# Where a decoder step splits its attention output, and where the taps of a short convolution stand on the vector engine

## The chip, the cores and the metric

The kernel runs on one core of one Trainium2 chip. The metric is the device time of one execution in microseconds (us), the median of several runs. TensorE does matrix products and transposes, VectorE (DVE) and ScalarE (ACT) do elementwise work, GpSimd (POOL) a little of it, and SyncE (SP) issues nearly all transfers. Each engine takes its instructions strictly in the order in which they are written, and semaphores order one engine against another.

## The reference, cut to what matters

One inference step of a two-layer decoder trunk, for 512 prompt tokens and 8 x 4 sample tokens (544 columns in all), everything in float32. Each layer is a feed-forward half step, a mixer, and a second feed-forward half step:

```
x = LN(alpha*x + 0.5*SwiGLU_1(x))
f_r, f_s, f_g = split(x @ W_in)          # 2696 columns: 22 chunks of 128
x = LN(alpha*x + W_out[concat(RWKV7(f_r), SWA(f_s), GDN(f_g))])
x = LN(alpha*x + 0.5*SwiGLU_2(x))
```

SWA is windowed attention (8 query heads). RWKV7 has 4 heads, taken in two pairs; GDN, a gated delta rule, has 4 heads in two more pairs. GDN's q, k and v go through a causal convolution over four tokens first:

```
conv = full[:, 0:T] * conv_w[0]
for j in range(1, 4): conv = conv + full[:, j:j+T] * conv_w[j]
q, k, v = split(silu(conv))
```

Each pair of heads then builds a 128 x 128 triangular system per token tile, inverts it, and runs a recurrence over the four tiles of 128 tokens.

## The kernel before

Activations lie with features on partitions and the 544 tokens along the free axis. Every float32 product of the large matrices is done as three products of a high and a low part (`xh`, `xl` of the activations, `wh`, `wl` of the weights). ACT makes the high part by a copy, DVE the low part by a subtraction.

The mixer of a layer starts with the projection: 22 chunks, each one weight block (`proj_chunk` on ACT and DVE, `proj_part` on TensorE). The steps of the prompt's attention are spread between the chunks; the last of them, `values(7)`, leaves the attention output `y_attn` complete two chunks before the end. Between the last two chunks ACT does two Tanh on `proj[:, 6]` (`lora_t`), which DVE then turns into the operand `lora` of the first products of RWKV (`zw`, `a_mm`).

After the projection comes `head_pairs`. Four pairs of heads, q = 0 to 3 (0 and 1 are RWKV, 2 and 3 are GDN), go through `prepare(q)` and `finish(q)`. Both are Python generators, one pair per engine, and `alternate` lays the steps of two of them into one program: the samples' attention (`samples_attend`, 7 steps) beside `prepare(0)`, then `prepare(q + 1)` (32 steps for q + 1 = 1, 30 for 2 and 3) beside `finish(q)` (22 steps). What stands in which step therefore decides the order on an engine; nothing is reordered on the chip.

Two places matter here.

1. The split of `y_attn` (128 x 2048). On ACT the copy to `xh` (`attn_h`) stands in the first step of `samples_attend`, on DVE the subtraction into `xl` (`attn_l`) does too. With the interleaving that is after `prepare(0)` has asked for the sum of squares `kk_sum`: on ACT behind the Ln and Exp of `rsqrt`, on DVE ahead of `newton`, whose first instruction (it ticks `kk_read`) lets TensorE go on with the third of the four `cum` products (L940). `y_attn` lies in the space that `prepare(0)` later uses for its tiles R_ to KT_; so only the exponentials of `cum` wait for `attn_l`.

2. The four taps of GDN's convolution (`tap(0)` to `tap(3)` in `prepare_gdn` on DVE; each is three instructions on about 512 columns and three on 32). Taps 0 to 2 stand in the first step of `prepare_gdn`, tap 3 at the head of the second. Also in the first step TensorE does the 4 `cum` and 16 `dif` products of the pair; behind them, in its own first step of `finish`, stand the first products of the recurrence (for q = 1), for whose result DVE's copy `cx` (L2328) waits. For q = 2 that copy is L2322 and waits for nothing that TensorE does here. ACT's Tanh (`conv_t`) wait for the whole convolution, and what follows from it (`conv_s`, the squares, `qk_sum`, `rsqrt`, `newton`, the grams, the inverse) is a chain through all three engines.

Of the kernel before, what the change touches and what calls it, by code (L numbers as in the profile page):

```python
# [17 lines left out]
F32 = mybir.dt.float32  # L18
# [242 lines left out]
def trunk(nc, A, O, layers=DEPTH):  # L261

    with ExitStack() as ctx:
# [106 lines left out]
        def region(o, w):  # L370
            return ar[:, o:o + w], o + w

        M_NORM = M_WORK + 6 * NT
        ck, _ = region(M_TMP, DEC_BATCH * P)
        y_attn, _o = region(M_TMP, 4 * NT)
        kd, _o = region(_o, 2 * NT)
        vt, _o = region(_o, TILES * P)
        ko, _o = region(_o, P)
        stat, _o = region(_o, 40)
        assert _o <= M_NORM  # L380
        vn, _o = region(M_NORM, DEC_BATCH * P)
# [935 lines left out]
        def _(act):  # L1317
# [91 lines left out]
            def one_layer(lay):  # L1409
# [61 lines left out]
                for g in range(PC):  # L1471
                    proj_chunk(g)
                    if g == FIRST_SHIFTED - 1:
                        double_keys()
                    if g == FIRST_ACTION - 2:
                        caches()
                    for action, s in actions_of(g + 1):
                        take(action, s)
                    if g == PC - 2:
                        act.wait_ge(sem("shifted"), at(lay, "shifted", 7))  # L1480
                        go(proj[0:32, 6, :], proj[0:32, 6, :], ACT.Tanh).then_inc(*tick("lora_t"))
                        go(proj[64:128, 6, :], proj[64:128, 6, :], ACT.Tanh, scale=0.5).then_inc(*tick("lora_t"))

                def samples_attend():

                    act.wait_ge(sem("proj_d"), at(lay, "proj_d", PC))
                    go(xe[:, :, :, 3:7], proj[:, GCH:GCH + 6, SEQ:NT].rearrange("p c (b t) -> p c b t", b=DEC_BATCH)).then_inc(*tick("xe"))
                    act.wait_ge(sem("y_copied"), at(lay, "y_copied", HALVES))
                    go(xh[:, 2:6, 0:SEQ], y_attn[:, :, 0:SEQ]).then_inc(*tick("attn_h"))
                    act.wait_ge(sem("tail_t"), at(lay, "tail_t", 3))  # L1490
# [45 lines left out]
                def prepare_rwkv(p):  # L1536
                    q, c, U, lwt = p.q, p.c, p.U, p.lwt
                    act.wait_ge(sem("attn_out"), at(lay, "attn_out", 32))
                    act.wait_ge(sem("ys"), at(lay, "ys", 1))
                    if q:  # L1540
                        act.wait_ge(sem("attn_l"), at(lay, "attn_l", 2))
                    if q == 1:
# [12 lines left out]
                    act.wait_ge(sem("cum"), at(lay, "cum", q + 1))  # L1555
                    act.wait_ge(sem("attn_l"), at(lay, "attn_l", 1))
                    go(U[:, 0:3, 0:SEQ].rearrange("p k (i n) -> p k i n", i=TILES),
# [216 lines left out]
        def _(dve):  # L1774
# [133 lines left out]
            def one_layer(lay):  # L1908
# [118 lines left out]
                for g in range(PC):  # L2027
# [6 lines left out]
                    for action, s in actions_of(g + 1):  # L2034
                        take(action, s)

                ts(par("a0h"), par("a0"), 0.5, None, ALU.mult, None).then_inc(*tick("ys"))
                ts(par("kah"), par("k_a"), 0.5, None, ALU.mult, None).then_inc(*tick("d_seq"))
# [4 lines left out]
                def samples_attend():  # L2043

                    dve.wait_ge(sem("qm_zero"), at(lay, "qm_zero", 1))
                    for h in range(8):
                        dve.tensor_copy(qm_d[64 * (h // 4):64 * (h // 4) + 64, :, h % 4 * 4:h % 4 * 4 + 4],
                                        proj[64 * (h % 2):64 * (h % 2) + 64, SCH + h // 2, SEQ:NT].rearrange("p (b t) -> p b t", b=DEC_BATCH)).then_inc(*tick("qm"))
                    dve.wait_ge(sem("attn_h"), at(lay, "attn_h", 1))
                    tt(xl[:, 2:6, 0:SEQ], y_attn[:, :, 0:SEQ], xh[:, 2:6, 0:SEQ].bitcast(F32), ALU.subtract).then_inc(*tick("attn_l"))  # L2050
                    yield
# [71 lines left out]
                def prepare_rwkv(p):  # L2123
# [3 lines left out]
                    dve.wait_ge(sem("attn_out"), at(lay, "attn_out", 32))  # L2127
                    if q:
                        dve.wait_ge(sem("attn_l"), at(lay, "attn_l", 2))
                    if q == 1:  # L2130
# [44 lines left out]
                def prepare_gdn(p):  # L2175
# [25 lines left out]
                    dve.wait_ge(sem("xe"), at(lay, "xe", 1))  # L2201
                    for k in range(3):
                        tap(k)
                        dve.wait_ge(sem("d_seq"), last(lay, "d_seq"))
                    yield
                    tap(3)
                    dve.wait_ge(sem("dif"), at(lay, "dif", 2 * c + 1))
                    for n in range(2):
                        ts(gram[:, 4 * n:4 * n + 4, 2 * P:3 * P], ps[:, 2 + n, :].rearrange("p (m n) -> p m n", m=4), 0.0, None, ALU.min, None).then_inc(*tick("dif_min"))
                    yield  # L2210
                    dve.wait_ge(sem("dif"), at(lay, "dif", 2 * c + 2))
                    ts(gram_s[:, :, 2 * NSAMP:3 * NSAMP], ps[0:NSAMP, 1, 0:2 * NSAMP].rearrange("p (m n) -> p m n", m=2), 0.0, None, ALU.min, None).then_inc(*tick("dif_min"))
                    yield
                    for n in range(3):
                        dve.wait_ge(sem("dif_e"), at(lay, "dif_e", 3 * c + n + 1))
                        gr, wd, mask = (gram[:, 4 * n:4 * n + 4], P, cst("gmask")) if n < 2 else (gram_s, NSAMP, cst("gmask_s", NSAMP))
                        for k in (1, 0):
                            tt(gr[:, :, (2 + k) * wd:(3 + k) * wd], gr[:, :, 2 * wd:3 * wd],
                               bc(mask[:, k * wd:(k + 1) * wd].rearrange("p (o n) -> p o n", o=1), [wd, gr.shape[1], wd]), ALU.mult).then_inc(*tick("d_seq"))
# [351 lines left out]
```

## Time and profile before

| | us |
|---|---|
| median of 3 runs | 2966.72 |
| lowest and highest of them | 2965.29, 2972.21 |
| the profiled execution | 2972.21 |
| its span in the trace | 2970.4 |
| mean granted clock of TensorE | 0.912 |

The profiled execution took 1.8 us more than its span and is the slowest of the three runs, 5.5 us over the median. The granted clock is given as a part of full speed: 1.0 is 2.4 GHz and 0.5 is 1.2 GHz, and a value between is a stretch with both. In the trace the mixer of the first layer runs from 606 to 1073 us and that of the second from 2070 to 2534 us; layer 1 is the second one in what follows, layer 0 the first.

### The profile page before, as it was taken

How to read it: one execution, taken by the hardware profiler on the slowest of the kernel's cores; microseconds unless marked ns; L12 is line 12 of the kernel's file. 1: busy time of each engine (PE TensorE's matmuls, PEld its weight loads, DVE VectorE, ACT ScalarE, POOL GpSimd, SP SyncE). 2: the span in 40 equal slices, each digit the busy share in tenths (PEclk: the TensorE clock that was granted, in tenths of full speed). 3: DMA queues.
4: the chain of work that ended last, by engine and by line, in shares of the span. 5: the costliest groups of instructions: out<-in, count | busy, mean ns of one | idle time of the engine just before them, and what ended most of it. 6: DMA issues, size and time to landing. Idle time of an engine off the chain costs nothing.

```text
span 2970.4 us, 59212 instructions
## 1 busy us (share of the span) xinstructions
PE 2726.1 (92%) x23222; PEld 2548.2 (86%) x23222; DVE 1668.4 (56%) x2503; ACT 947.0 (32%) x1694; POOL 161.1 (5%) x168
## 2 busy tenths in 40 slices
PE   8999999879796989999999999998887778999997
PEld 8999998866665889999999999987666667999996
DVE  5666347744646466663366653566445654666534
ACT  4333233422212243332233332343122222433323
POOL 1030110000000010001100001100000000100011
PEclk9999999976767999999999999999767779999998
DMA  4842334100000322232232222431000012223221
GB/s 113 101 91 87 89 103 128 44 27 1 9 9 1 95 68 86 85 90 86 76 88 87 85 86 87 119 101 51 7 1 9 9 42 73 79 86 90 82 87 60
DMA packets 380501, 201.67 MB, mean 68 GB/s; under 512 B 41461, under 2 KB 376821, under 8 KB 379528
## 3 DMA queue, kind: packets, MB, share of 16 engines
q1 hardware_dynamic: 377928, 197.46, 23.1%
q0 software_dynamic: 2400, 1.82, 1.9%
q8 instruction: 118, 1.93, 0.3%
q14 instruction: 55, 0.45, 0.0%
HBM read 188.07 MB, written 13.34 MB: 68 GB/s over the span
## 4 chain that ended last, share of the span: by engine, by line
PE 78%; DVE 10%; issue 5%; ACT 4%; DMA 1%; SPq 1%; DVEq 0%; POOLq 0%; ACTq 0%; POOL 0%
PE ps L682 52%; PE ps L737 25%; DVE ar L1920 3%; ACT ar L1415 2%; DVE ar L1914 2%; DVE wl L1798 1%; ACT wh L1346 1%; SPq L529 1%; PE ps L1011 1%; DVE x L1914 1%; DMA raws<-in_ffn_w_in 0%; DVE xl L1905 0%; DVE ar L1950 0%; DVE ar L1917 0%; DMA raws<-in_w_in 0%
## 5 line engine op out<-in xcount | busy, mean ns | idle before, releaser
L1798 DVE TENSOR_TENSOR wl<-raws,wh 128x1024 fp32r<-128x1024 f32 x336 | 411.2, 1225 | 671.1 <-ACT wh L1346 666.8
L737 PE MATMUL ps<-ar 64*64 64x64 f32 (+13 forms) x5408 | 508.7, 287 | 127.3 <-ACT ar L1415 39.0
L682 PE MATMUL ps<-xh,wh 128*128 128x272 f32 x2880 | 604.5, 291 | 19.9 <-DVE wl L1798 17.4
L682 PE MATMUL ps<-xh,wl 128*128 128x272 f32 x2880 | 599.5, 290 | 0.0
L682 PE MATMUL ps<-xl,wh 128*128 128x272 f32 x2880 | 598.0, 289 | 0.0
L737 PEld LDWEIGHTS ps<-ar 64*64 64x64 f32 (+6 forms) x5408 | 380.8, 172 | 231.1 <-issue 71.3
L1346 ACT ACTIVATE wh<-raws 128x1024 fp32r<-128x1024 f32 x336 | 354.8, 1057 | 416.3 <-PE ps L682 375.4
L682 PEld LDWEIGHTS ps<-xh,wh 128*128 128x128 f32 x2880 | 457.0, 190 | 23.0 <-DVE wl L1798 19.4
L682 PEld LDWEIGHTS ps<-xl,wh 128*128 128x128 f32 x2880 | 457.3, 190 | 0.0
L682 PEld LDWEIGHTS ps<-xh,wl 128*128 128x128 f32 x2880 | 456.8, 190 | 0.0
L682 PE MATMUL ps<-hh,wh 128*128 128x272 f32 x1408 | 292.2, 289 | 0.0
L682 PE MATMUL ps<-hl,wh 128*128 128x272 f32 x1408 | 290.4, 287 | 0.0
L682 PE MATMUL ps<-hh,wl 128*128 128x272 f32 x1408 | 290.1, 287 | 0.0
L1415 ACT ACTIVATE ar<-ps 64x256 f32<-64x256 f32 (+19 forms) x250 | 91.2, 392 | 481.5 <-PE ps L737 379.4
L682 PEld LDWEIGHTS ps<-hl,wh 128*128 128x128 f32 x1408 | 222.1, 188 | 0.0
L737 PE MATMUL ps<-xh,wh 128*128 128x272 f32 (+1 forms) x896 | 204.3, 310 | 18.4 <-DVE xl L1914 13.3
L682 PEld LDWEIGHTS ps<-hh,wl 128*128 128x128 f32 x1408 | 219.8, 188 | 0.0
L682 PEld LDWEIGHTS ps<-hh,wh 128*128 128x128 f32 x1408 | 219.7, 188 | 0.0
L737 PE MATMUL ps<-xl,wh 128*128 128x272 f32 (+1 forms) x896 | 190.6, 295 | 0.0
L737 PE MATMUL ps<-xh,wl 128*128 128x272 f32 (+1 forms) x896 | 190.3, 294 | 0.0
L737 PEld LDWEIGHTS ps<-xh,wh 128*128 128x128 f32 x896 | 146.5, 196 | 37.0 <-issue 28.4
L1375 ACT ACTIVATE hh<-work 128x544 f32 (+1 forms) x88 | 58.0, 660 | 370.4 <-DVE work L1862 370.4
(188 smaller groups left out, 2735.5 us busy)
## 6 DMA issues: line engine op xcount, KB each, us to landing
raws<-in_ffn_w_in SPq DMA_DIRECT2D x176, 512.0 KB, 3.7
raws<-in_ffn_w_out SPq DMA_DIRECT2D x64, 512.0 KB, 4.0
raws<-in_w_in SPq DMA_DIRECT2D x42, 512.0 KB, 3.7
raws<-in_ffn_w_out SPq DMA_DIRECT2D x32, 384.0 KB, 3.4
raws<-in_w_out SPq DMA_DIRECT2D x16, 448.0 KB, 4.0
x_kept<-x SPq DMA_DIRECT2D x2, 2176.0 KB, 10.1
x<-x_kept SPq DMA_DIRECT2D x2, 2176.0 KB, 8.0
ar<-in_consts SPq DMA_DIRECT2D x2, 1337.5 KB, 6.7
```

The costliest lines, as they stand in the source:

```text
L529: sp.dma_start(dst, src, allow_slow_non_contiguous=slow).then_inc(*tick(name, 16))
L682: ins = pe.matmul(ps[:, bank + h, 0:n1 - h * NH], w[u % 2][:, k, :], a[:, k0 + k, h * NH:n1], start=(first and k == 0 and n == 0), stop=(l ...
L737: return pe.matmul(dst, lhsT, rhs, start=start, stop=stop, **kw)
L1011: ins = pe.transpose(ps[0:w, i % 4, s * P:(s + 1) * P], src[:, o:o + w], ident)
L1346: act.activation(wh[u % 2][:, :, :], raw[u % 2][:, :, :], ACT.Copy).then_inc(sem("wh_done"), 1)
L1375: act.activation(chunk(hh, i * 2 + u), work[:, 2 + u, :], ACT.Copy).then_inc(sem("hh_done"), 1)
L1415: return act.activation(dst, src, fn, **kw)
L1798: dve.tensor_tensor(wl[u % 2][:, :, :], raw[u % 2][:, :, :], wh[u % 2][:, :, :].bitcast(F32), ALU.subtract).then_inc(sem("wl_done"), 1)
L1914: return dve.tensor_tensor(out, a, b, op)
L1920: return dve.scalar_tensor_tensor(out=out, in0=a, scalar=x, in1=b, op0=o1, op1=o2)
```

## The change

The change has three parts. `y_attn` gets a place of its own further up in memory (what is saved is that it no longer shares space with the cached keys `ck`; it now overlaps the tiles BT to GATE of `prepare(0)`, and the first step of `prepare(0)` waits for `attn_l` on both engines). The split of `y_attn` moves from `samples_attend` to directly behind the projection, on ACT ahead of the two Tanh of `lora_t`, which move there as well, and on DVE ahead of the three small scalings and of `lora`. And the taps of GDN's convolution are spread over four steps.

```diff
@@ regions @@
-        ck, _ = region(M_TMP, DEC_BATCH * P)
-        y_attn, _o = region(M_TMP, 4 * NT)
+        ck, _o = region(M_TMP, DEC_BATCH * P)
         kd, _o = region(_o, 2 * NT)
...
         stat, _o = region(_o, 40)
+        y_attn, _o = region(_o, 4 * NT)
@@ ACT, projection @@
                     for action, s in actions_of(g + 1):
                         take(action, s)
-                    if g == PC - 2:
-                        act.wait_ge(sem("shifted"), at(lay, "shifted", 7))
-                        go(proj[0:32, 6, :], proj[0:32, 6, :], ACT.Tanh).then_inc(*tick("lora_t"))
-                        go(proj[64:128, 6, :], proj[64:128, 6, :], ACT.Tanh, scale=0.5).then_inc(*tick("lora_t"))
+
+                act.wait_ge(sem("y_copied"), at(lay, "y_copied", HALVES))
+                go(xh[:, 2:6, 0:SEQ], y_attn[:, :, 0:SEQ]).then_inc(*tick("attn_h"))
+                act.wait_ge(sem("shifted"), at(lay, "shifted", 7))
+                go(proj[0:32, 6, :], proj[0:32, 6, :], ACT.Tanh).then_inc(*tick("lora_t"))
+                go(proj[64:128, 6, :], proj[64:128, 6, :], ACT.Tanh, scale=0.5).then_inc(*tick("lora_t"))
@@ ACT, samples_attend @@
-                    act.wait_ge(sem("y_copied"), at(lay, "y_copied", HALVES))
-                    go(xh[:, 2:6, 0:SEQ], y_attn[:, :, 0:SEQ]).then_inc(*tick("attn_h"))
@@ ACT and DVE, prepare_rwkv @@
-                    if q:
-                        act.wait_ge(sem("attn_l"), at(lay, "attn_l", 2))
+                    act.wait_ge(sem("attn_l"), at(lay, "attn_l", 1 if q == 0 else 2))
...
-                    act.wait_ge(sem("attn_l"), at(lay, "attn_l", 1))
@@ DVE, projection and samples_attend @@
+                dve.wait_ge(sem("attn_h"), at(lay, "attn_h", 1))
+                tt(xl[:, 2:6, 0:SEQ], y_attn[:, :, 0:SEQ], xh[:, 2:6, 0:SEQ].bitcast(F32), ALU.subtract).then_inc(*tick("attn_l"))
                 ts(par("a0h"), par("a0"), 0.5, None, ALU.mult, None).then_inc(*tick("ys"))
...
-                    dve.wait_ge(sem("attn_h"), at(lay, "attn_h", 1))
-                    tt(xl[:, 2:6, 0:SEQ], y_attn[:, :, 0:SEQ], xh[:, 2:6, 0:SEQ].bitcast(F32), ALU.subtract).then_inc(*tick("attn_l"))
@@ DVE, prepare_gdn @@
-                    for k in range(3):
-                        tap(k)
-                        dve.wait_ge(sem("d_seq"), last(lay, "d_seq"))
-                    yield
-                    tap(3)
+                    tap(0)
+                    yield
+                    dve.wait_ge(sem("d_seq"), last(lay, "d_seq"))
+                    tap(1)
                     dve.wait_ge(sem("dif"), at(lay, "dif", 2 * c + 1))
...
                     yield
+                    dve.wait_ge(sem("d_seq"), last(lay, "d_seq"))
+                    tap(2)
                     dve.wait_ge(sem("dif"), at(lay, "dif", 2 * c + 2))
...
                     yield
+                    dve.wait_ge(sem("d_seq"), last(lay, "d_seq"))
+                    tap(3)
                     for n in range(3):
                         dve.wait_ge(sem("dif_e"), at(lay, "dif_e", 3 * c + n + 1))
```

The rows that follow are the instructions of an engine in program order, with the semaphore that one waits for behind it.

The first place is VectorE where the projection ends and `prepare(0)` begins, before the change. The 64x544 row is `lora`, the one behind it the first product of `prepare(0)`; TensorE waits for `lora`.

```order
L1914 TENSOR_TENSOR ar<-ar,work 128x544 [waits proj_e]
L1917 TENSOR_SCALAR ar<-ar 128x2 x3
L1917 TENSOR_SCALAR ar<-ar 64x544 [waits lora_t]
L2127 ISA
L1917 TENSOR_SCALAR ar<-ar 128x544 [waits attn_out]
```

And with the change:

```order
L1912 TENSOR_TENSOR ar<-ar,work 128x544 [waits proj_e]
L2035 REGISTER_ALU
L1912 TENSOR_TENSOR xl<-ar,xh 128x4x512 [waits attn_h]
L1915 TENSOR_SCALAR ar<-ar 128x2 x3
L1915 TENSOR_SCALAR ar<-ar 64x544 [waits lora_t]
L2125 ISA
L1915 TENSOR_SCALAR ar<-ar 128x544 [waits attn_l,attn_out]
```

The low half of the attention output, `xl`, now stands ahead of `lora`. Before, it stood ahead of the instruction that ticks `kk_read`, the one that waits for `rs_exp`:

```order
L2047 COPY ar<-ar 64x8x4 x7
L1914 TENSOR_TENSOR xl<-ar,xh 128x4x512 [waits attn_h]
L2075 REGISTER_ALU
L1920 SCALAR_TENSOR_TENSOR ar<-ps,ar 128x544 [waits rs_exp]
L1920 SCALAR_TENSOR_TENSOR ar<-ar 128x544 [waits kk_read]
```

The second place is ScalarE at the same point, with the change. The xh row is the copy of the attention output, the two behind it are the Tanh of `lora_t`, which stood one projection chunk earlier before.

```order
L1425 REGISTER_ALU
L1415 ACTIVATE ar<-ar,cols 128x544 [waits proj_n]
L1480 ISA
L1415 ACTIVATE xh<-ar 128x4x512 [waits y_copied]
L1482 ISA
L1415 ACTIVATE ar<-ar 32x544 [waits shifted]
L1415 ACTIVATE ar<-ar 64x544
L1538 ISA
L1539 ISA [waits attn_out]
L1415 ACTIVATE ar<-ar 128x544 [waits attn_l,ys]
```

What moved is again the 128x4x512 operation, to ahead of everything that `prepare(0)` asks for.

The third place is VectorE in `prepare(2)` beside `finish(1)`, with the change. The COPY from ps is the recurrence's `cx`, the row above it the last of tap 0; before, the fifteen rows of taps 1 and 2 and their waits stood between these two.

```order
L1915 TENSOR_SCALAR ar<-ar 128x512
L1915 TENSOR_SCALAR ar<-ar 128x32
L2324 REGISTER_ALU [waits state_out]
L2328 COPY ar<-ps 128x128 [waits cx]
L2201 REGISTER_ALU
L1918 SCALAR_TENSOR_TENSOR ar<-ar 128x511 [waits d_seq]
L1918 SCALAR_TENSOR_TENSOR ar<-ar 128x32
```

All of taps 1, 2 and 3 now stands behind the copy; of the old order only tap 3 did.

## Rows read from the trace of the kernel before

**Rows 1.** The page's first part: busy time of each engine, share of the span.
```profile
PE 2726.1 (92%) x23222; PEld 2548.2 (86%) x23222; DVE 1668.4 (56%) x2503; ACT 947.0 (32%) x1694; POOL 161.1 (5%) x168
```

**Rows 2.** Stretches: mixer of layer 0; prepare(2) of either layer. Length, busy times, clock.
```profile
core 0: us, PE busy (x) PEld busy (x) DVE busy (x) ACT busy (x) POOL busy (x), PEclk, DMA share, GB/s
606.00:1073.60 467.60, 383.02 (x3947) 309.22 (x3948) 245.94 (x512) 120.62 (x220) 12.23 (x9) 0.74 0.09 24
794.60:899.20 104.60, 86.18 (x905) 66.56 (x905) 57.08 (x125) 23.83 (x46) 0.00 (x0) 0.66 0.03 7
2258.80:2356.80 98.00, 78.62 (x905) 60.95 (x905) 56.40 (x125) 23.83 (x46) 0.00 (x0) 0.74 0.03 7
```

**Rows 3.** Chain of waits behind layer 1's projection: start us, length us, what.
```profile
2072.41 3.83 PE ps L737 x14
...
2082.22 1.79 ACT xh L1415
...
2086.24 0.72 DVE ar L1920
2087.01 3.57 PE ps L737 x6
```

**Rows 4.** Timeline of VectorE there: start us, us, line, operation, idle before.
```profile
2071.59 1.30 DVE L1917 TENSOR_SCALAR ar<-ar 128x2 f32<-128x2 f32 x5
...
2084.03 2.29 DVE L1914 TENSOR_TENSOR xl<-ar,xh 128x2048 fp32r<-128x2048 f32 x1 [2.37 <-ACT xh L1415]
```

**Rows 5.** Timeline of ScalarE there.
```profile
2066.36 1.32 ACT L1415 ACTIVATE ar<-ar 32x544 f32<-32x544 f32 x2
...
2072.36 0.73 ACT L1415 ACTIVATE ar<-ar 128x544 f32<-128x544 f32 x1
...
2082.11 1.89 ACT L1415 ACTIVATE xh<-ar 128x2048 fp32r<-128x2048 f32 x1
```

**Rows 6.** TensorE's cum products: layer 0 (the first two rows), then layer 1.
```profile
618.82 1.75 PE L737 MATMUL ps<-ar 128*128 128x386 f32 x4
623.40 1.01 PE L737 MATMUL ps<-ar 128*128 128x386 f32 x1 [2.84 <-DVE ar L1920]
...
2081.38 1.46 PE L737 MATMUL ps<-ar 128*128 128x386 f32 x4
```

**Rows 7.** One stretch there, same columns as in Rows 2.
```profile
2080.00:2084.00 4.00, 2.85 (x17) 1.64 (x15) 1.44 (x9) 3.99 (x5) 0.00 (x0) 0.96 0.00 0
```

**Rows 8.** Timeline of VectorE in prepare(2) of layer 0.
```profile
797.05 5.16 DVE L1920 SCALAR_TENSOR_TENSOR ar<-ar 128x511 f32<-128x511 f32 x12
803.70 0.29 DVE L2328 COPY ar<-ps 128x128 f32<-128x128 f32 x1 [1.48 <-PE ps L737]
803.90 2.55 DVE L1920 SCALAR_TENSOR_TENSOR ar<-ar 128x509 f32<-128x509 f32 x6
...
810.98 2.63 DVE L1920 SCALAR_TENSOR_TENSOR ar<-ar 128x544 f32<-128x544 f32 x4
```

**Rows 9.** Timeline of TensorE there.
```profile
795.25 8.01 PE L737 MATMUL ps<-ar 128*128 128x256 f32 x40 [5.84 <-DVEq L2200]
803.10 0.56 PE L737 MATMUL ps<-raws,gram_odd 128*128 128x64 f32 x4
```

**Rows 10.** Chain of waits behind it: start us, length us, what.
```profile
811.74 1.30 ACT ar L1415 x2
813.04 0.14 issue
813.18 3.98 PE ps L737 x8
...
820.80 1.30 DVE ar L1920
```

**Rows 11.** Timeline of TensorE in prepare(3) of layer 0.
```profile
899.92 9.71 PE L737 MATMUL ps<-ar 128*128 128x256 f32 x54 [5.84 <-DVEq L2200]
```

**Rows 12.** VectorE there.
```profile
907.00 0.23 DVE L2322 COPY ar<-ar 128x128 f32<-128x128 f32 x1
...
909.61 1.28 DVE L1917 TENSOR_SCALAR ar<-ps 128x512 f32<-128x512 f32 x2
```

**Rows 13.** TensorE from 908.4 us on, by form: count, busy us, mean ns.
```profile
L737 PE MATMUL ps<-ar 128*128 128x128 f32 x1 | 0.3, 275 | 0.0
```

More of the change, by code:

```diff
@@ L2127, in prepare_rwkv @@
                     dve.wait_ge(sem("attn_out"), at(lay, "attn_out", 32))
-                    if q:
-                        dve.wait_ge(sem("attn_l"), at(lay, "attn_l", 2))
+                    dve.wait_ge(sem("attn_l"), at(lay, "attn_l", 1 if q == 0 else 2))
                     if q == 1:
```

## The prediction

> **What bounds the kernel now.** I read the busy times first, then the chain of waits, then the timelines of the three engines where the change puts its hand, and the granted clock by stretches last. TensorE is busy for 92% of the span [rows 1], so over the whole run it is the bound. But the change touches only the mixers, and there the picture is another: the mixer of layer 0 takes 467.6 us at a mean granted clock of 0.74, with TensorE busy 383 of them and VectorE 246 [rows 2]. No engine is full; what sets the time is one chain through TensorE, ACT and DVE. The reader should see in [rows 3] and [rows 10] that pieces of all three engines follow each other without a hole, so that whatever is put ahead of one of them on its own engine is paid in full, and what is put beside them is free.
>
> **Part one: the split of the attention output.** Before, the chain behind layer 1's projection goes: DVE makes `lora`, TensorE starts `zw` at 2072.41, and later ACT's copy `attn_h` (1.79 us), DVE's `attn_l` behind it, DVE's 0.72 us that tick `kk_read`, and TensorE's third `cum` product at 2087.01 [rows 3]. Both large operations are on the path there. After, they are on the path earlier. ACT is free for `attn_h` at 2072.36, where it now starts its next operation [rows 5]. `attn_l` starts 1.92 us after `attn_h` (2084.03 - 2082.11) [rows 4, 5] and holds DVE for 2.21 us, until the next start at 2086.24 [rows 3, 4]. From the first of the small scalings to the start of `zw` it is 0.82 us (2072.41 - 2071.59) [rows 3, 4]. The two Tanh, 1.32 us together [rows 5], now come behind `attn_h` and end near 2075.5, hidden by `attn_l`, which ends near 2076.5. So `zw` starts at 2072.36 + 1.92 + 2.21 + 0.82 = 2077.3, which is 4.9 us late. Nothing else for TensorE stands ahead of `zw` in its queue, so it idles.
>
> Against that the later delay goes. In layer 1 TensorE had done the first two `cum` products at 2081.38 + 1.46 = 2082.84 and waited to 2087.01 [rows 3, 6]. Without the split `kk_read` follows the Exp, which ended before `attn_h` began at 2082.11 [rows 5], so 0.72 us later TensorE is no longer kept waiting: it goes on at 2082.84 + 4.9 = 2087.7, a net loss of 0.7 us. In layer 0 the first two end at 618.82 + 1.75 = 620.57 and the third starts at 623.40 [rows 6]; it will start at 625.5, a net loss of 2.1. Together +2.8 us. The ACT wait on `attn_l` that now stands at the head of `prepare(0)` holds up a Square of 0.73 us [rows 5], which ends at 2077.2 and is wanted only after `zw` and `a_mm` (3.83 us [rows 3]): hidden. The copies of the samples' last rows come later in absolute time, but so does all that wants them.
>
> The price has two ends. If the wait for `kk_read` were replaced by another of the same length, the 4.9 us of both layers stay: +9.8. If the products behind it run faster, it is less. The first two products (772 columns) took 1.46 us, the rest with 876 columns 3.57 [rows 3, 6]: the second group ran at the lower level (1.2 GHz), the first at the upper (0.96 granted in that stretch [rows 7]). TensorE stood still between them. Without that pause the rest may keep the upper level and take 1.8 less in each layer: +2.8 - 3.6 = -0.8, and somewhat more if the next products keep it too, so -4 at the low end. I take +2.8, the rows as they stand.
>
> The Trainium skill (TensorE: Matmul & The Clock Gate, Part 4: PE-mode transpose) says that transposes do not count as work that lifts TensorE's clock. Ahead of these `cum` products stand sixteen transposes, so by that rule they would run low after the change, and +2.8 holds. The row of the stretch with transposes and `cum`, 0.96 granted, does not bear the rule out here; without it the sum would lean to -0.8.
>
> **Part two: the taps.** For q = 2, layer 0: TensorE starts `cum` and `dif` at 795.25 and ends them at about 803.1, where the first product of the recurrence follows [rows 9]. DVE meanwhile did tap 0 (until 797.05) and taps 1 and 2 (5.16 us, until 802.2), idled 1.48 us, copied `cx` at 803.70 and went on with tap 3 at 803.90 [rows 8]. Three taps were hidden by TensorE. After, the copy stands behind tap 0, and it can't come earlier than 803.70, since TensorE's order is the same and so are its operands. DVE idles from 797.05 to 803.70, and taps 1 and 2 are done behind it. From 803.90 to 810.98, when `conv_s` begins, DVE has no idle time at all: [rows 8] give the first and the last operation of that stretch, and each of those between begins where the one before it ends. So `conv_s` begins 5.16 us late. It is on the chain: ACT's squares follow at 811.74, TensorE's sums at 813.18, ACT's `rsqrt`, DVE's `newton` at 820.80 [rows 10]. The recurrence does not gain from it, since its copies and its state update on DVE stand at the same steps as before and behind more work. +5.16 us.
>
> For q = 3 the copy `cx` waits for nothing of TensorE's in this stretch; before, it stood at 907.00 behind the taps [rows 12], after 5.16 us earlier. But its reader on TensorE stands behind the same `cum` and `dif`, started at 899.92 [rows 11]: at 908.4 the last `dif` product of 0.275 us is still running [rows 13], so `dif` is ready at about 908.55. Before, DVE took it up at 909.61, behind tap 3 [rows 12]; after, it takes it up at 908.6, 1.0 us earlier, having done only taps 0 and 1 and idled some 4 us. Taps 2 and 3 (2.58 and 2.55 [rows 8]) then come behind. Net +5.1 - 1.0 = +4.1 us. By the bounds of the moment at which `dif` is ready (908.2 to no gain at all) 3.7 to 5.1.
>
> Nothing covers these: ACT's Tanh wait for the whole convolution, and DVE does the masks meanwhile as before. Both layers: 2 x (5.16 + 4.1) = +18.5 us, bounds 17.8 and 20.6.
>
> **The sum.** +18.5 + 2.8 = +21.3 us. The profiled execution took 2972.2, so it would take 2993.5. It lies 5.5 over the median of the runs; on the median, 2966.7 + 21.3 = 2988.0 us, slower by 0.7%.
>
> **What the clock may add.** The same `prepare(2)` with `finish(1)`, the same 905 products, took 104.6 us at a granted clock of 0.66 in layer 0 and 98.0 at 0.74 in layer 1 [rows 2]. So the phase in which TensorE's activity meets the clock is worth 6.6 us in one layer's stretch, and any shift throws that die anew. I count 6.6 us either way as the noise of one such stretch.
>
> **The rivals.**
> A: the clock falls further. TensorE now waits 5 us longer at six places (before `zw`, and before the sums of q = 2 and 3, in two layers). For it: after such waits these rows show low stretches (0.66 and 0.74 over `prepare(2)`). Against it: TensorE was at the lower level behind these waits already. If all stretches of `prepare(2)` lose another 0.08 in both layers, that is 2 x 6.6 on top: 3001 us. The Trainium skill (TensorE: Matmul & The Clock Gate, Why this matters for your kernels) states that rule, that gaps between matmul bursts take TensorE back to the lower clock; it speaks against this change, and the trace agrees in kind.
> B: the taps cost nothing on balance. The state copy of q = 3 comes 5.1 us earlier; if the recurrence rather than the convolution set the time of that stretch, q = 3 would win what q = 2 loses: 2966.7 + 2.8 = 2969.5, no measurable change. For it: DVE's copies of the recurrence do lie on the chain elsewhere. Against it: TensorE is in `dif` until 908.5 whatever DVE does, and the chain runs through the squares and sums [rows 10]. A part of the same case is that the change does not do what it says: that DVE is not reordered on the chip as written; the order of the program leaves no room for it.
> C: faster. The one mechanism is the clock: 0.08 more of it gave 6.6 us. To go under 2957.8, 30 us must come back, 15 in a layer, that is a granted clock up by 0.18 in `prepare(2)` of both (0.84 and 0.92), or the like spread over `prepare(3)`. At 0.90 in both stretches it would be 20 + 13 us back: 2955. It decides only from a clock of some 0.88 on, and with longer pauses nothing points there.
>
> **How the numbers follow.** The forecast, 2988, gets 0.72, with a range of its own from 2974 (18.5 - 4 - 7 above the median) to 2996; A 0.16; B 0.08; C 0.04. The range that should hold 8 in 10 reaches from 2973 to 3003, leaving out B, C and the tail of A. 0.3% of the time, 8.9 us, is about what a measurement of this kernel can tell from no change: faster 0.04 (C), within it 0.09 (B and the lowest part of the forecast), slower 0.87.
>
> **What would show it.** Right: `zw` starts 7.3 us instead of 2.5 behind the last projection product; TensorE's wait inside `cum` is gone; DVE idles about 6.6 us ahead of the copy at L2328 in `prepare(2)` and about 4 us ahead of the two minima in `prepare(3)`, where it idled 1.5 and 0; `conv_s` of q = 2 begins 19.1 us behind the end of tap 0, where it was 13.9 (797.05 to 810.98). Wrong: if the idle time before `cx` is short, TensorE was not the releaser; if all that is there and the time is still below 2975, the clock rose, and the stretches' granted clock must say so; if the total is over 3003, look for stretches below 0.66.

## The result and the profile after

The changed kernel takes 3005.4 us (median of 4 runs, 2995.5 to 3008.2), the kernel before 2966.0 in the same comparison (4 runs, 2962.7 to 2972.2): +39 us, ratio 1.0125, 95% interval 1.0096 to 1.0153, so slower by some 1.3%. The forecast was +21 us. The profiled execution took 3005.6 us, its span is 3003.8, 33.4 us more than the span of the profiled execution before.

Busy times, which answer to [rows 1]:

```profile
PE 2742.8 (91%) x23222; PEld 2561.6 (85%) x23222; DVE 1669.7 (56%) x2503; ACT 949.2 (32%) x1694; POOL 161.5 (5%) x168
```

TensorE does the same 23222 products and is busy 16.7 us longer with them. DVE and ACT gain 1 and 2 us. So about half of the 33.4 us between the two profiled executions is not waiting but slower products.

The stretches answering to [rows 2] (columns as there), mixer of layer 0 and prepare(2) of either layer:

```profile
606.00:1087.00 481.00, 386.59 (x3946) 312.40 (x3946) 245.93 (x512) 122.34 (x221) 11.93 (x9) 0.72 0.08 23
794.60:906.00 111.40, 88.11 (x905) 68.28 (x905) 56.90 (x125) 24.32 (x46) 0.00 (x0) 0.64 0.03 6
2272.90:2384.00 111.10, 88.11 (x905) 68.32 (x905) 56.57 (x125) 24.32 (x46) 0.00 (x0) 0.64 0.03 6
```

Both layers now take 111 us at 0.64, where before one took 104.6 at 0.66 and the other 98.0 at 0.74. They have become equal: the slow one, plus the 5.0 us of later work shown below, plus another 1.5 to 1.8.

TensorE behind layer 0's projection and then layer 1's, answering to [rows 3, 6] (start, length, what, idle before):

```profile
613.21 4.74 PE L737 MATMUL ps<-ar 32*128 32x128 f32 x14 [7.44 <-DVE ar L1915]
...
623.53 3.15 PE L737 MATMUL ps<-ar 128*128 128x386 f32 x10
```

```profile
2091.17 4.74 PE L737 MATMUL ps<-ar 32*128 32x128 f32 x14 [7.44 <-DVE ar L1915]
...
2101.50 3.15 PE L737 MATMUL ps<-ar 128*128 128x386 f32 x10
```

`zw` starts behind a wait of 7.44 us. The ten `cum` records (of which the prediction's first two products are four) run through in 3.15 us, with no wait inside.

VectorE in prepare(2), answering to [rows 8]:

```profile
803.73 0.29 DVE L2328 COPY ar<-ps 128x128 f32<-128x128 f32 x1 [6.73 <-PE ps L737]
803.94 2.56 DVE L1918 SCALAR_TENSOR_TENSOR ar<-ar 128x511 f32<-128x511 f32 x6
...
810.40 2.54 DVE L1918 SCALAR_TENSOR_TENSOR ar<-ar 128x509 f32<-128x509 f32 x6
...
815.96 2.63 DVE L1918 SCALAR_TENSOR_TENSOR ar<-ar 128x544 f32<-128x544 f32 x4
```

The idle time ahead of the copy is 6.73 us (1.48 before). The last row is `conv_s`: 815.96, before 810.98, at equal start of the stretch.

VectorE and TensorE in prepare(3), answering to [rows 11, 12]:

```profile
906.71 8.12 PE L737 MATMUL ps<-ar 128*128 128x256 f32 x54 [5.84 <-DVEq L2197]
...
913.72 1.29 DVE L1915 TENSOR_SCALAR ar<-ps 128x512 f32<-128x512 f32 x2 [2.64 <-PE ps L737]
```

The minima come 7.0 us behind TensorE's start (9.7 before) and `cum` and `dif` take 8.12 us instead of 9.71.

**A ledger by product.** Both traces hold the same 23222 products in the same order, so the starts of each one can be subtracted. The lag of the changed kernel, counted from the first product of each trace, is 0.9 us in layer 0's projection, -0.4 at the head of prepare(2) (TensorE's wait ahead of `cum` and `dif`), 4.6 at the sums of q = 2, 6.4 at the head of prepare(3), 8.7 at the recurrence's product behind the third tap there, and 13.3 at the mixer's end; the FFN adds 0.1. In layer 1 the same six places read 13.4, 13.4, 18.3, 26.8, 29.0 and 32.2. The steps of 5.0 and 2.3 us are later work on VectorE. The rest of the loss stands in two stretches. The first goes from the first sum of q = 2 to the last product ahead of prepare(3)'s wait, 823 records; the second from that recurrence's product of q = 3 to the first one behind the mixer. Here they are for the kernel before, layer 0 and 1, first stretch and then second, and under it the same four of the changed kernel:

```profile
813.20:893.90 80.70, 72.82 (x823) 55.15 (x823) 35.86 (x78) 16.37 (x31) 0.00 (x0) 0.66 0.04 9
2277.40:2351.50 74.10, 65.21 (x823) 49.50 (x823) 35.24 (x78) 16.41 (x31) 0.00 (x0) 0.76 0.04 9
914.10:1121.70 207.60, 177.69 (x1672) 158.69 (x1673) 112.09 (x175) 64.71 (x104) 13.38 (x9) 0.88 0.21 62
2371.70:2580.80 209.10, 179.58 (x1672) 159.34 (x1673) 112.08 (x175) 64.70 (x104) 13.21 (x9) 0.86 0.21 61
```

```profile
818.10:900.60 82.50, 74.63 (x822) 56.78 (x823) 35.86 (x78) 16.37 (x31) 0.00 (x0) 0.63 0.04 8
2296.10:2378.60 82.50, 74.66 (x822) 56.83 (x823) 35.87 (x78) 16.37 (x31) 0.00 (x0) 0.63 0.04 8
923.10:1135.40 212.30, 182.92 (x1672) 161.88 (x1673) 112.48 (x175) 64.60 (x103) 13.40 (x9) 0.85 0.21 60
2401.10:2613.40 212.30, 182.84 (x1672) 161.81 (x1673) 112.40 (x175) 64.61 (x103) 13.39 (x9) 0.85 0.21 60
```

The reader should see that length and granted clock go together (74.1 at 0.76, 80.7 at 0.66, 82.5 at 0.63), while DVE and ACT are busy as long as ever. This is where the surplus over the forecast is. The experiments ask why. Each length is that of one profiled execution.

### The profile page after: what moved, and what is told of

The parts are those of the page before. It is cut to its first block, busy times and chain, and to the rows that moved or that the text cites. A ratio compares the mean times of both kernels' runs of the same rounds, so it can differ in the third digit from the quotient of the medians.

```text
span 3003.8 us, 59208 instructions
## 1 busy us (share of the span) xinstructions
PE 2742.8 (91%) x23222; PEld 2561.6 (85%) x23222; DVE 1669.7 (56%) x2503; ACT 949.2 (32%) x1694; POOL 161.5 (5%) x168
## 4 chain that ended last, share of the span: by engine, by line
PE 78%; DVE 10%; issue 5%; ACT 4%; DMA 1%; SPq 1%; DVEq 0%; POOLq 0%; ACTq 0%; POOL 0%
PE ps L682 51%; PE ps L737 25%; DVE ar L1918 3%; DVE ar L1912 2%; ACT ar L1415 2%; DVE wl L1796 1%; ACT wh L1346 1%; SPq L529 1%; PE ps L1011 1%; DVE x L1912 1%; DMA raws<-in_ffn_w_in 0%; DVE xl L1903 0%; DVE ar L1948 0%; ACT xh L1415 0%; DMA raws<-in_w_in 0%
## 5 line engine op out<-in xcount | busy, mean ns | idle before, releaser
L737 PE MATMUL ps<-ar 64*64 64x64 f32 (+13 forms) x5408 | 517.6, 292 | 146.3 <-ACT ar L1415 39.0
L737 PEld LDWEIGHTS ps<-ar 64*64 64x64 f32 (+6 forms) x5408 | 388.7, 177 | 250.2 <-issue 71.8
L737 PE MATMUL ps<-xh,wh 128*128 128x272 f32 (+1 forms) x896 | 204.1, 310 | 18.4 <-DVE xl L1912 13.3
```

The costliest lines, as they stand in the source:

```text
L737: return pe.matmul(dst, lhsT, rhs, start=start, stop=stop, **kw)
```

## The experiments

All ratios are to the kernel before, run beside them; a ratio of 1.001 is 3.0 us. "First stretch" and "second stretch" are those above, layer 0 / layer 1 of the profiled run.

**The change taken apart.** e1 is the change without the spread taps (that is, `y_attn` in its own place and the early split), e2 the spread taps alone; e3 and e4 spread the taps in one head pair (code shortened):

```
+ late = c == 0        # e3; e4: c == 1
  tap(0)
+ if not late: tap(1), tap(2) here, tap(3) behind the yield, as before
+ else: tap(1), tap(2), tap(3) one behind each of the next yields, as changed
```

e1: 

> The kernel before with the early split of the attention output alone (part one), the taps where they were. Theory T (the loss is all in the taps; the split is free): 2966 +- 4 us, with zw about 4.9 us later and the wait for kk_read gone, net -1.3 to 0 us in each layer as in the profile of the changed kernel. The prediction's own term: +2.8 us, 2969. Rival S (the longer wait ahead of zw also costs granted clock): +8 us or more, 2974 and up, with more time at the lower level behind zw.


Measured 1.0010 [0.9999, 1.0021]; first stretch 74.1 / 74.0. The split is nearly free, +3 us with an interval from 0 to 6. S, which wanted 8 or more, falls.

e2: 

> The kernel before with the spread taps alone (part two). Theory T: as slow as the changed kernel, 3000 to 3008 us, the clock lower as there (0.901 against 0.912). Rival S (part of the clock's loss hangs on the split's wait ahead of zw): 2985 to 2995. The prediction's own term, path alone: 2966 + 18.5 = 2984.5.


Measured 1.0127 [1.0109, 1.0145]; 82.5 / 82.5, second stretch 212.3 / 212.4. The whole loss is in the taps. S falls again.

e3: 

> The taps spread in prepare(2) alone. Path alone: 2 x 5.1 = +10.2 us, 2976. If the lateness in prepare(2) brings its own loss of clock, as the ledger of the changed kernel reads (1.4 us in layer 0 and 8.1 in layer 1 inside prepare(2)): 2966 + 10.2 + 9.5 = 2986. If the two late steps cost clock only together: 2976.


Measured 1.0083 [1.0067, 1.0099], +25 us; 82.5 / 82.4, second stretch 207.8 / 207.9. Path alone falls: each layer pays another 6 to 8 us behind the sums.

e4: 

> The taps spread in prepare(3) alone. Path alone, from the rows of the changed kernel (the third gap 4.9 us longer, 1.5 us given back ahead of it): 2 x 3.4 = +6.8 us, 2973; the prediction's +4.1 each would be 2974. If the lateness in prepare(3) brings the clock's loss behind it (4.6 us in layer 0, 1 to 2.4 in layer 1): 2966 + 6.8 + 6.3 = 2979. If both halves cost as much as both together, e3 + e4 = the changed kernel's +39.


Measured 1.0052 [1.0037, 1.0067], +15 us; first stretch 74.0 / 74.0, second 212.7 / 208.9. The path of q = 3 grew by 3.8 us in each layer. The second stretch, 207.6 and 209.1 us before, accounts for another 5 of the rest.

**Is it lateness as such?** In e5 and e7 the taps stay, and VectorE repeats mask products behind the masks of prepare(2), 8 or 4 of them (code shortened):

```
+ if c == 0:
+     for r in range(8):      # e7: 4; e10: 7
+         wait for d_seq; tt(gram[..., 3 * P:4 * P], same, gmask, ALU.mult)
```

e5: 

> The kernel before, taps as they were, with eight more copies of a mask product on VectorE (0.62 us each, without effect on the result) behind the masks of prepare(2): everything that the spread taps delay there is late by about the same 5 us, by other work. Theory L (lateness at this place costs granted clock, whatever makes it): as slow as the kernel with spread taps in prepare(2) alone, +26 us, 2990, and the stretch from the wait ahead of cum and dif of q = 2 to that of q = 3 takes 117 to 118 us instead of 104. Rival R (the loss comes from the reordering itself, the later copies of the recurrence or the later Exp and masks): path alone, 2 x 5 = +10, 2974, and 109 us. Rival P (the phase decides by chance): the two layers differ by 6 us or more.


Measured 1.0048 [1.0034, 1.0062], +14 us.

```profile
816.00:894.20 78.20, 69.51 (x822) 53.33 (x823) 35.81 (x78) 16.34 (x31) 0.00 (x0) 0.68 0.04 9
2283.70:2361.90 78.20, 69.44 (x821) 53.27 (x822) 35.85 (x77) 16.38 (x31) 0.00 (x0) 0.68 0.04 9
```

The sums came 5.9 us late (each extra product took 0.73), yet only 78.2 us follow, not 82.5. L falls as it was put. R is not decided here: the path alone, 2 x 5.9 us, would be 1.0040, inside the interval, and 78.2 lies between the two lengths on time, 74.1 and 80.7. My rival P expected unequal layers; they are equal.

e7: 

> As the kernel with eight extra mask products, but with four: about 2.5 us late. Theory L in proportion: half the loss, +13 us, 2977, stretch 111. If the clock is lost at a threshold between 0 and 5 us of lateness: either path alone, +5, 2969 and 106.7 us, or the whole loss, +5 + 17 = 2986 and 115. Theory P (phase): any value, without order among 0, 2.5 and 5 us.


Measured 1.0021 [1.0010, 1.0032], 2.9 us late, 77.9 / 77.9. In proportion? 2.9 late costs 77.9, 5.9 late 78.2, 5.0 late 82.5: there is no order in it. The total alone would fit the path, 5.8 us.

**Is it TensorE's longer wait?** e6 is e3 with products nobody reads in the wait; e8 is the kernel before with such products in two other waits (code shortened):

```
+ def fill(bank, count): mm(ps[:, bank, NH:512], cst("blk"), cst("gd")[:, 0:512 - NH])  # count times
+ if c == 0: fill(0, 6)                    # e6, ahead of the wait for the state
+ banks_free(q); fill(0, 7); wait for ge   # e8, q = 2 and 3
```

e6: 

> The kernel with spread taps in prepare(2) alone (2990 us), with six products of 240 columns on TensorE whose result nobody reads, put where it waits 5.5 us for the recurrence's state ahead of the sums of q = 2. Theory W (the longer wait itself takes the clock): the wait is filled, the clock behind it is as before, 117.5 us become about 109 in each layer, 2990 - 17 = 2973. Rival M (the work behind the wait meets the clock's steps at another moment, and filling changes little): 2986 to 2994. Rival H (the products run at the lower level and end behind the wait): up to 1 us later in each layer.


Measured 1.0065 [1.0051, 1.0079], +19 us, which is not clear of e3's +25; first stretch 79.3 / 82.5. Of the wait of 5.5 us 1.2 to 1.3 are left. In layer 1 the clock did come up as the filling ended (1.00 from 2276.2 to 2279.4 us), and was back at the lower level when the sums began at 2280.2. Filled or not, layer 1 pays the full 82.5. W falls as the main cause.

e8: 

> The kernel before with seven products of 240 columns that nobody reads at the head of prepare(2) and prepare(3), where TensorE waits 5.85 us for ge ahead of cum and dif (40 and 54 products, 8.0 and 9.7 us, the first 5 us of them at the lower level). Theory W (waiting takes the clock, work brings it back): the clock has risen when cum and dif begin, they take 3 us less, four times: -12 us, 2952, or better if the next stretch rises too. Rival M: the clock is no better, 2964 +- 3. Rival H: the seven end late, up to +1 us each, 2968.


Measured 0.9965 [0.9955, 0.9975], 10 us faster than the kernel before, and the fastest of all versions. TensorE in prepare(2) of layer 0:

```profile
791.84 4.76 PE L737 MATMUL ps<-ar 128*128 128x240 f32 x14 [0.56 <-ACT ar L1420]
797.13 5.57 PE L737 MATMUL ps<-ar 128*128 128x256 f32 x40 [0.53 <-DVEq L2205]
```

`cum` and `dif` take 5.57 us instead of 8.01 [rows 9]; the sums come 1.4 us earlier and the first stretch is 74.8 / 76.4. So W holds for the products right behind the filled wait. At q = 3 nothing is gained: the recurrence's product comes 14.2 us behind the start of `cum`, as before. Twice 1.4 and the stretches explain some 5 of the 10 us. In layer 1 the products from `zw` to the head of prepare(2) took 180.2 us, where layer 0 and the kernel before have 186.8 to 187.0; that is one layer of one execution, so the rest stays open.

**The moment.**

e10: 

> As the kernel with eight extra mask products in prepare(2) (5.85 us late in the trace, 0.73 us each), but with seven: 5.1 us late, which is what the spread taps make. The stretch from the sums of q = 2 to the head of prepare(3), the same products in all kernels, took 74.0 us on time, 77.9 at 2.9 us late, 78.2 at 5.85 and 82.5 with the spread taps. Theory P (what the clock takes depends only on the moment at which the work behind the wait comes): about 82.5 in both layers, total 2964 + 10 + 17 = 2990 by the medians of the first comparison. Theory R (the spread taps themselves, by the order of the copies and Exp, cost the clock): 78.2, total 2982.


Measured 1.0060 [1.0039, 1.0081], +18 us:

```profile
821.80:904.20 82.40, 74.51 (x822) 56.71 (x823) 35.80 (x78) 16.31 (x31) 0.00 (x0) 0.63 0.04 8
2292.90:2375.30 82.40, 74.50 (x822) 56.72 (x823) 35.87 (x78) 16.38 (x31) 0.00 (x0) 0.63 0.04 8
```

One extra product fewer than e5, 0.8 us earlier at the sums, and 4.2 us slower behind them in each layer: the very number of the spread taps, with the taps where they were. R falls by these rows; the totals of e5 and e10, +14 and +18 us, can't be told apart.

e11, which is e3 with one extra mask product: 

> The taps spread in prepare(2) alone, and one extra mask product (0.73 us) behind the masks: 5.7 us late instead of 5.0. Theory P (moment alone): the stretch behind the sums falls from 82.5 to about 78.2 us though the work is later, total 2990 - 6 = 2984. Theory R (order of the work): it stays at 82.5, total 2991 to 2992.


Measured 1.0033 [1.0020, 1.0047], +10 us where e3 had +25:

```profile
819.10:893.80 74.70, 66.04 (x823) 50.56 (x823) 35.57 (x78) 16.33 (x31) 0.00 (x0) 0.74 0.04 9
2283.40:2358.10 74.70, 66.04 (x823) 50.51 (x823) 35.60 (x78) 16.38 (x31) 0.00 (x0) 0.74 0.04 9
```

More work on the path, and the kernel is 15 us faster. P gave the direction; the stretch is even 3.5 us shorter than it said.

e12, which is e8 with `fill(0, 3)` ahead of the small cum: 

> The kernel before with seven unused products at the heads of prepare(2) and prepare(3) (-10.6 us already measured) and three more ahead of the small cum, where TensorE waits 2.4 us for the recurrence. Theory W (work in the waits keeps the higher level): the stretch up to the sums shortens by another 1 to 2 us and the sums run high (4.5 us at the lower level become 3): another -4 to -8 us, 0.994 of the kernel before. Rival H (three products of 0.4 to 0.8 us push the small cum and ACT's Exp behind it): no gain over the version with seven, 0.9965, or worse by up to 4 us.


Measured 0.9997 [0.9983, 1.0010]: the gain of e8 is gone. Neither theory had it: W wanted more gain, and H a loss of at most 4 us against e8. The first stretch was 74.7 / 74.7 and the sums came 0.15 us later than in e8, so H's mechanism isn't in the rows either, and where the 9 us went stays open.

e13, six mask products in prepare(3) (`c == 1`): 

> The kernel before with six extra mask products (0.73 us each, 4.4 us) in prepare(3) only. Path alone: 2 x 4.4 = +8.8 us, and the stretch from the recurrence's product behind it to the end of the mixer stays at 207.7 us. Theory L (the lateness brings the clock's loss at q = 3): it takes 212.3 as with the spread taps, total +18. Theory R (order of the work): 207.7, total +9.


Measured 1.0046 [1.0031, 1.0061], +14 us; 4.4 us late, second stretch 210.2 / 210.3. Between the two: the clock takes 2.3 us, neither 0 nor 4.6. Its first stretch, untouched, took 80.6 / 80.7.

**The whole change with the moment moved.** The changed kernel and `range((1, 1)[c])` (e14) or `range((1, 2)[c])` (e15) extra mask products.

e14: 

> The changed kernel with one extra mask product without effect (0.73 us) on VectorE behind the masks of prepare(2), and one behind those of prepare(3). Theory P (the clock's part depends on the moment): the stretch behind the sums of q = 2 falls from 82.5 us to about 74.7 in both layers, which is -15.6 + 1.5; with prepare(3) unchanged but for 0.7 us in each layer the total is 3005 - 12.7 = 2993 (ratio 1.008), and if prepare(3) also falls from 212.3 to 207.7, 2983 (ratio 1.005). Rival R (the loss belongs to the order of the work): 2.9 us slower than the changed kernel, 3008.


Measured 1.0069 [1.0044, 1.0095], 2986.8 us, against 1.0125 [1.0096, 1.0153] for the change as it is.

```profile
820.50:895.40 74.90, 66.16 (x823) 50.53 (x822) 35.62 (x78) 16.29 (x32) 0.00 (x0) 0.74 0.04 9
2288.20:2362.90 74.70, 66.00 (x823) 50.38 (x823) 35.61 (x78) 16.27 (x31) 0.00 (x0) 0.74 0.04 9
918.60:1126.90 208.30, 178.48 (x1675) 159.32 (x1676) 112.23 (x176) 64.58 (x103) 13.37 (x9) 0.88 0.22 61
2386.30:2601.40 215.10, 185.48 (x1675) 163.93 (x1674) 112.53 (x176) 64.58 (x103) 13.39 (x9) 0.84 0.21 59
```

Two superfluous operations of 0.73 us in each layer make the changed kernel some 17 us faster (5 to 28 by the two intervals). P holds for q = 2; R falls.

e15: 

> As the kernel with one and one extra product on top of the change, but two (1.46 us) in prepare(3). Theory P: the stretch behind the recurrence's product of q = 3 takes another length than with one, by more than the 0.1 us that equal kernels differ by, and either of the two, not in order of lateness, is the longer. Rival Q (q = 3 pays a fixed price, 212.3 us, whatever the moment): both 212 to 213, and the total 1.5 us over the version with one.


Measured 1.0072 [1.0044, 1.0101]; 74.8 / 74.7, second stretch 209.2 / 207.7. Q falls: q = 3 has no fixed price, it went from 207.7 to 215.1 in these two kernels.

e16, the kernel before with one mask product in prepare(2): 

> The kernel before with one extra mask product (0.73 us) in prepare(2). The stretch behind the sums took 74.0 us in five profiled layers with these steps on time and 80.7 in three, so on time lies at a border. Theory P: 0.7 us later it lies clear of the border, 74 to 75 or 80 to 81 in both layers; by the first the total is that of the kernel before or 1 to 3 us less in spite of more work (ratio 0.999 to 1.0), by the second +6 to +9 (1.003). Rival (path alone): +1.5, 1.0005.


Measured 1.0005 [0.9990, 1.0021]; 76.5 / 76.6. Equal layers, as P says, but neither of the two values I named.

e17, e8 with that product: 

> The kernel before with seven unused TensorE products at the heads of prepare(2) and prepare(3) (ratio 0.9965) and one extra mask product (0.73 us) in prepare(2). The stretch behind the sums took 74.9 and 76.4 us there. Path alone: +1.5 us, 0.997. Theory P: another value of that stretch, 74 to 82, the same in both layers; total between -3 and +15 against the version without the extra product.


Measured 1.0008 [0.9994, 1.0022]; 78.0 / 78.1, second stretch 214.5 / 213.3. One operation of 0.73 us takes e8's gain away. Its profiled run was its slowest (2983.9 of 2962.8 to 2983.9), so the second stretch need not be typical.

**What the sixteen give together.** The first stretch against the moment at which the sums begin, reckoned from TensorE's wait at the head of prepare(2) and against the kernel before:

```
-1.4 us (e8)      74.8, 76.4      +2.9 (e7)             77.9, 77.9
-1.2    (e12)     74.7, 74.7      +5.0 (after, e2, e3)  82.4 to 82.5, six layers
-0.7    (e17)     78.0, 78.1      +5.1 (e6, filled)     79.3; +5.0: 82.5
 0      (before)  80.7, 74.1      +5.1 (e10)            82.4, 82.4
+0.7    (e16)     76.5, 76.6      +5.7 (e11, e14, e15)  74.7 to 74.9, six layers
                                  +5.9 (e5)             78.2, 78.2
```

The traces show one thing more about this moment. In all 30 profiled layers with nothing added ahead of `cum` (every kernel but e8, e12 and e17) the granted clock goes up 5.0 to 5.3 us behind the start of `cum` and down again 11.9 to 12.2 us behind it. So a moment counted from there is also a moment counted from the clock's changes. What follows differs in how long the clock stays down. Here are the long stretches wholly at the lower level (0.50), of the kernel before in layer 0 and 1, then of the changed kernel, e10 and e11 in layer 0 (columns PE, PEld, DVE, ACT, POOL as in [rows 2]):

```profile
820.80:861.60 40.80, 36.85 (x282) 27.47 (x284) 20.78 (x41) 4.92 (x15) 0.00 (x0) 0.50 0.00 1
2285.20:2305.50 20.30, 18.71 (x84) 13.43 (x86) 10.97 (x20) 2.47 (x7) 0.00 (x0) 0.50 0.00 0
807.40:854.90 47.50, 35.43 (x161) 25.08 (x162) 26.74 (x60) 12.96 (x24) 0.00 (x0) 0.50 0.00 1
810.80:858.30 47.50, 35.21 (x160) 24.92 (x161) 26.52 (x54) 12.55 (x24) 0.00 (x0) 0.50 0.00 1
807.50:841.20 33.70, 20.89 (x94) 15.18 (x95) 21.97 (x44) 12.41 (x22) 0.00 (x0) 0.50 0.00 0
```

The two layers of the kernel before, 80.7 and 74.1 us, part only in this: the same low stretch lasts twice as long in layer 0.

In eight profiled layers on time (before, e1, e4, e13) the first stretch took 74.0 to 74.1 us five times and 80.6 to 80.7 three times, 76.5 on average. With that average, 207.9 us for the second stretch on time, and the measured lateness, the sums of the kernels come out as follows, in us over the kernel before (reckoned, measured): e2 35, 38; e3 22, 25; e4 13, 15; e5 15, 14; e7 9, 6; e10 22, 18; e11 8, 10; e13 13, 14; e14 22, 21; e16 1.5, 1.5. So path and these two stretches give the measured totals within their intervals (e15, 17 and 21, too); only e8 (-5, -10) and e17 (14, 2) lie outside. The agreement is rougher than it looks. Each kernel has one profiled execution, the fastest of e1 and e4 and the slowest of e10 and e17, and executions of one kernel lie up to some 20 us apart. And other stretches move without an edit in them: from `zw` to the head of prepare(2) the kernels without the early split took 180.2 to 187.1 us.

## Why the prediction was wrong, point by point

**Part one: right in mechanism, small in size.** `zw` later by 4.9 us: 613.21 - 608.47 = 4.7, with the lag of the products ahead 4.9 in both layers. The wait for `kk_read` gone: yes, and nothing took its place. Net: the end of `cum` lies 0.2 us earlier in layer 0 (forecast +2.1) and 0.2 later in layer 1 (forecast +0.7), both from the projection's end. The rest of `cum` did keep the upper level, as my low bound had it (the ten records took 3.15 us at a granted 1.00, before 1.75 + 3.62 in layer 0 with the wait between, the last six at 0.50). The rule that transposes do not lift the clock, weighed in the prediction from the Trainium skill (TensorE: Matmul & The Clock Gate, Part 4: PE-mode transpose), would have had them run low behind sixteen transposes. The changed kernel speaks against its use here: the granted clock is 0.50 over the four records ahead of the transposes (618.7 to 620.7 us) and 1.00 over `cum` (from 623.5), and what ran between is the transposes. e1's +3 [0, 6] holds the forecast's +2.8 as well as zero.

**Part two, q = 2: right.** Forecast +5.16; measured 815.96 - 810.98 = 4.98, and 5.0 us at TensorE's sums in both layers.

**Part two, q = 3: right in kind, too high for the changed kernel.** Forecast +4.1, bounds 3.7 to 5.1. With nothing changed ahead (e4) it is 3.8 in both layers. In the changed kernel it is 2.3: `cum` and `dif` met the upper level sooner (8.12 us instead of 9.71), so `dif` was ready 7.0 us behind their start and not 8.6, and VectorE idled 2.64 us ahead of the minima where the forecast had about 4.

The path terms sum to 2 x (5.0 + 2.3) = 14.6 and the split's 0 to 6, where the forecast had 21.3. With the 3.8 of e4, where nothing ahead of q = 3 had changed, they are 17.6 and the split's 0 to 6, which holds the forecast. So the path was forecast about right, and the miss lies in the clock.

**The step that failed: "What the clock may add".** I read off the profile that the same 905 products took 98.0 or 104.6 us, called it noise of "6.6 us either way", and left it out of the sum. Three things were wrong with that. First, with the changed kernel's lateness it is no noise: the stretch has one length, to 0.2 us, in both layers and in several kernels (82.4 to 82.5 in eight layers with e10, and 74.7 to 74.9 in six at +5.7). So it does not average out over the layers but doubles. It is not so at every moment: on time it is 74.1 or 80.7, and e6 and e8 have unequal layers. Second, it is not symmetric: the 74.0 us that most layers on time had is the shortest of all values seen, and 82.5 the longest. Third, it has a partner behind q = 3 (207.9 on time, 212.3 after). Together 2 x (6.0 + 4.4) = 21 us, which with the 14.6 is 35 of the 39 measured. The prediction's own sign came true: over 3003 us, stretches below 0.66.

**Rival A**, at 0.16, named the right place (low clock in prepare(2)) and nearly the right time, 3001; the stretch did fall below 0.66. Its cause, that the longer waits take the clock, is not what the runs showed: e6 filled the wait and layer 1 paid all the same, and e11 has a longer wait than e3 and lost nothing. The rule of the Trainium skill that I put beside it (TensorE: Matmul & The Clock Gate, Why this matters for your kernels), that gaps take TensorE back, agrees in kind with e8, where work in a gap made the products behind it 2.4 us shorter; it does not say which change pays. **B** falls: VectorE was idle as forecast, and the taps alone cost 38 us (e2). **C** falls: the clock went down.

That the length of the first stretch hangs on the moment at which the sums begin, and not on the order of the work or on the amount of lateness, is shown by e10, e11 and e14; for the second stretch e15 against e14 says as much, with one execution each. How the chip chooses between its two levels from it isn't settled by these runs, and why the kernel before falls on either 74.1 or 80.7 isn't either.

## What to carry over

Where a stretch is bound by TensorE and the trace has it at two lengths with two granted clocks, put both into the sum as ends of one term, multiplied by the number of layers, before pricing any wait. Leave room beyond the ends as well: 82.5 lay outside both 74.1 and 80.7. Before you believe that an edit of some us is good or bad there, run it with a superfluous operation of under 1 us beside it: here that was worth 15 us, more than the edit's own path (10). And subtract the starts of like products in the two traces: it separates waits from slower products in one table.

## What was not expected of the hardware

One operation of 0.73 us more on VectorE made the kernel 15 us faster (e3 to e11), and one fewer made the first stretch 4 us longer in each layer (e5 to e10). The granted clock went with it, from 0.63 to 0.74 and from 0.68 to 0.63, while VectorE and ScalarE were as busy as before. Unused products on TensorE ahead of a burst shortened it from 8.01 to 5.57 us (e8).
